# Order of a VectorE queue in the softmax rounds of a two-layer encoder trunk: maximum and preparation piece exchanged

## The reference

```python
def one_block(q_blk):                       # 2 blocks of 128 queries, 8 heads, 2 softmaxes (c)
    s = jnp.einsum('bqhcd,bkhcd->bhcqk', q_blk, k).astype(jnp.float32) * scale
    p = jax.nn.softmax(s, axis=-1)
    a = p[:, :, 0] - lam * p[:, :, 1]
    return jnp.einsum('bhqk,bkhe->bqhe', a.astype(v.dtype), v)
...
f = lb_dir + (1.0 - lb_dir) * jax.nn.sigmoid(f_raw)     # HGRN2, each of two directions
k, logf = heads(1.0 - f), heads(jnp.log(f))             # the scan then takes cumsum(logf)
```

## Time and profile before

| | |
|---|---|
| median of three executions | 2962.78 us (2958.91 to 2967.27) |
| profiled execution, time | 2959.23 us |
| profiled execution, span in the trace | 2957.4 us |
| TensorE busy | 2665.2 us, 90% of the span |
| VectorE busy | 1923.5 us, 65% |
| ScalarE busy | 1073.4 us, 36% |
| rounds 0 to 15 of the attention | from 616.71 us to 703.58 us of the span |

### The profile page before, as it was taken

One profiled execution on the slowest core, in us unless ns is written; L12 is line 12 of the kernel. 1 busy time (PEld: TensorE's weight loads), 2 busy tenths in 40 slices (PEclk: granted clock), 3 DMA queues, 4 the chain that ended last, 5 costly groups with the idle time before them and its releaser, 6 DMA issues.

```text
span 2957.4 us, 41913 instructions
## 1 busy us (share of the span) xinstructions
PE 2665.2 (90%) x16522; PEld 2154.3 (73%) x16522; DVE 1923.5 (65%) x1948; ACT 1073.4 (36%) x858; POOL 128.9 (4%) x201
## 2 busy tenths in 40 slices
PE   6969999976769899999999976859979999999997
PEld 3438888733458688888888862548868888888886
DVE  7956666657935777677777756746676665555555
ACT  3333333343223333333444422023433333344442
POOL 1020000000000200000000021010020000000000
PEclk9989999977879999999999988979989999999999
DMA  7988878622235488787878759468837777555551
GB/s 249 349 269 271 288 257 288 214 72 69 73 109 176 170 277 273 257 286 262 285 261 293 279 158 227 157 174 276 284 124 230 235 231 236 187 195 187 184 185 57
DMA packets 289270, 639.65 MB, mean 216 GB/s; under 512 B 76370, under 2 KB 79316, under 8 KB 285588
## 3 DMA queue, kind: packets, MB, share of 16 engines
q1 hardware_dynamic: 239236, 584.44, 59.7%
q0 software_dynamic: 11008, 35.99, 4.1%
q10 hardware_dynamic: 38928, 17.86, 2.2%
HBM read 614.24 MB, written 19.79 MB: 214 GB/s over the span
## 4 chain that ended last, share of the span: by engine, by line
PE 79%; DVE 12%; ACT 3%; ACTq 2%; issue 2%; DMA 1%; SPq 1%; DVEq 0%
PE PS L267 46%; PE PS L268 23%; PE PS L220 2%; ACT Pb L939 2%; DVE Pb L1693 2%; DVE acc L1688 1%; PE PS L885 1%; ACTq L983 1%; PE PS L184 1%; PE PS L714 1%; DMA omat<-WF 1%; DVE wlo L257 1%; DVE HF L1612 1%; ACTq L416 1%; PE PS L735 1%
## 5 line engine op out<-in xcount | busy, mean ns | idle before, releaser
L267 PE MATMUL PS<-H,whi 128*128 128x512 f32 x5888 | 2077.1, 398 | 102.0 <-DVE wlo L257 78.1
L268 PE MATMUL PS<-H,wlo 128*128 128x256 f32 x5888 | 1653.1, 281 | 0.0
L267 PEld LDWEIGHTS PS<-H,whi 128*128 128x128 f32 x5888 | 1112.3, 189 | 369.5 <-DVE wlo L257 84.5
L257 DVE TENSOR_TENSOR wlo<-raw,whi 128x2048 fp32r<-128x2048 f32 x368 | 843.6, 2293 | 735.3 <-ACT whi L253 734.8
L253 ACT ACTIVATE whi<-raw 128x2048 fp32r<-128x2048 f32 x368 | 705.3, 1918 | 1255.9 <-PE PS L268 1215.1
L268 PEld LDWEIGHTS PS<-H,wlo 128*128 128x128 f32 x5888 | 1118.6, 190 | 0.0
L176 DVE SCALAR_TENSOR_TENSOR acc<-araw,cact,acc 128x1024 f32<-128x1024 f32 x240 | 307.4, 1281 | 1.4 <-DMA araw<-in_ada_w 1.0
L939 ACT ACTIVATE Pb<-PS 128x1024 f32 (+5 forms) x117 | 118.3, 1035 | 162.1 <-issue 75.8
L939 ACT ACTIVATE H<-Pb 128x512 fp32r (+2 forms) x142 | 95.1, 670 | 41.6 <-DVE Pb L1358 27.7
L1406 DVE TENSOR_TENSOR H<-Pb,H 128x512 fp32r<-128x512 f32 x128 | 87.6, 684 | 0.0
L1302 DVE TENSOR_TENSOR raw<-Pb,HF 128x1024 f32<-128x1024 f32 x64 | 74.1, 1220 | 9.9 <-DMA omat<-WF 7.0
(11 more groups left out here) (258 smaller groups left out, 1406.0 us busy)
## 6 DMA issues: line engine op xcount, KB each, us to landing
raw<-in_mlp_w SPq DMA_DIRECT2D x256, 1024.0 KB, 5.8
araw<-in_ada_w SPq DMA_DIRECT2D x276, 512.0 KB, 4.5
raw<-in_mix_w_in SPq DMA_DIRECT2D x64, 1024.0 KB, 7.7
raw<-in_s_w_glu SPq DMA_DIRECT2D x32, 1024.0 KB, 7.4
acc<-in_ada_w SPq DMA_DIRECT2D x44, 512.0 KB, 7.0
raw<-in_ada_w POOLq DMA_DIRECT2D x32, 512.0 KB, 4.1
raw<-in_mix_w_out SPq DMA_DIRECT2D x16, 1024.0 KB, 5.1
vmat<-Pb ACTq DMA_DIRECT2D x8, 1024.0 KB, 7.5
```

The lines of the kernel that those rows point to most:

```text
L257: nc.vector.tensor_tensor(wlo[:, s % 2, :], raw[:, s, :], whi[:, s % 2, :].bitcast(F), ALU.subtract).then_inc(S("lo_done"), 1)
L267: nc.tensor.matmul(PS[:, b, :], w[0], H2[:, :, k, :], start=first, stop=False, skip_group_check=True)
L268: return nc.tensor.matmul(PS[:, b, 0:T], w[1], H2[:, 0, k, :], start=False, stop=last, skip_group_check=True)
```

## The change

The order of two calls in VectorE's loop over the rounds is exchanged. The instructions, their data and their semaphores stay the same. Maxima are taken in rounds 0 to 13 only; rounds 14 and 15 issue the same order as before.

```diff
             for n in range(16):
                 mix(n)
+                between(n)
                 if n < 14:
                     row_max(n + 2)
-                between(n)
```

## The result

The changed kernel took 2939.26 us in the median of 14 executions, the kernel before 2959.07 us in 14 beside it; the ratio is 0.9948, with a 95% interval of 0.9927 to 0.9968. That is 15.4 us less by the ratio (0.0052 x 2959), 19.8 by the medians. So the question is whether the rounds saved more than was worked out, whether something behind them saved too, or whether the absolute time was wrong for another reason.

A forecast was written before the change was run, and what follows sets the result against it. VectorE was taken as the loop of the rounds, with one trip to TensorE inside. Waits of 21.8 us gone less 8.9 new give 12.9 us; 2962.8 - 12.9 was rounded to 2950 us, range 2944 to 2959.

The forecast's parts named there:

- The bound and the trip: Rounds: VectorE is the loop with one trip to TensorE; covering it with the piece removes 14 waits, 20.2 us.
- The far bound of 0.60 us for the gap: Gap from mixing to piece: taken as 0.15 us each; at 0.60 it would cost 6.3 us more.
- The short covers: Rounds 0 and 1: the piece ends before the scores are ready, leaving waits of 0.60 and 0.75 us.
- TensorE keeps up: From round 2: TensorE's 3.53 us at full clock fits VectorE's shortest round of 3.77, 0.24 us to spare.
- The rule of the Trainium skill: Transposes do not engage the full clock; the rival with low clock throughout the rounds gives 2972 us, chance 0.03.
- The wait for the logarithms: At the piece of round 9: VectorE's wait for ScalarE's logarithms grows from 1.57 to 4.81 us.
- TensorE's late rest of round 9: After the logarithms: some 4 us of TensorE's low-clock work left; under 1 us might show, counted as nothing.
- The sum of the rounds: Up to the mixing of round 14: 21.8 us gone, 8.9 new, net 12.9 us.
- The shift goes through: Behind the rounds: the whole 12.9 us shift reaches the end; rival that it is given back, 2963 us, chance 0.09.
- the time that I give: Whole kernel: median of the runs, 2962.8 us, less 12.9, rounded to 2950 us; forecast's chance 0.74.

The follow-up runs named there:

- load: Two 4x256 products added on TensorE behind gate_part each round: on the changed kernel 2951.32 us, stage 76.6; on the kernel before 2961.31 us, stage 86.9.
- the last two experiments: On the changed kernel: round 9 left in the old order, 2932.69 us; ScalarE's logarithms moved behind the copy of round 9, median 2949.49 us, ratio 0.9959.
- the filler: Changed kernel with the clearing memset of round 15 issued 8 times instead of once, ahead of the first level: median 2961.68 us, ratio 1.0007.

## Why the prediction was wrong, point by point

**The bound and the trip: right.** VectorE was the loop with one trip to TensorE in it; 1.41 us from mixing to piece was forecast and measured, 3.77 us for the shortest round against 3.71. The far bound of 0.60 us for the gap appeared only where it was before, ahead of L1550.

**The short covers: right in place, 0.4 us too small.** Round 0 waited 0.71 us (0.60 forecast). Round 1 waited 1.05 (0.75), since `gate_part(0)`, where the clock rises, took 2.66 us instead of 2.32; over the six traces with the new order in round 0 and no load this wait lies between 0.81 and 1.30 us.

**TensorE keeps up: right.** The clock stayed up through rounds 2 to 8 and no maximum waited there. The shortest round left TensorE 0.20 us idle (at 654.94), where I had 0.24. The rule of the Trainium skill that spoke against it ("TensorE: Matmul & The Clock Gate", Part 4) did not decide: with two transposes among 14 matmuls the granted clock was 1.00 in rounds 2 to 8 and 0.89 over the stage, not 0.50. That the room hangs on the clock is shown by the run with only odd rounds exchanged: where the clock fell in an exchanged round, the next one gave 1.1 us back.

**The wait for the logarithms: right.** 4.81 us forecast, 4.96 measured. I let TensorE's late rest of round 9 cost nothing, which held only because the scans stand in front of the next maximum; the last two experiments showed that it is the bound there.

**The sum of the rounds: 12.9 us forecast, 13.04 measured. The shift goes through: right** as far as 14.0 +- 3.3 us over all executions and the filler can tell.

**The step that failed is the last one: "the time that I give is 2962.8 - 12.9, rounded to 2950".** The median of three executions was taken as the kernel's time, and "each median moves by some us by itself" was not put into the range in its full size. Over 53 executions the kernel before has a mean of 2956.9 us, 5.9 less than that median. Less the measured 13.0 it gives 2943.9, already at the low end of the range; the changed kernel's 36 executions have 2943.0, and the median of the first 14 lay another 3.7 us lower. So of the 10.6 us between the unrounded 2949.9 and the measured 2939.3, the base is 5.9, the size of the change 0.1, and 4.6 are scatter, 0.9 of the mean of the 36 and 3.7 of that first median. The mechanism and its size were right, the base of the sum was mis-sized by 6 us, and the spread around it was taken too small.

## What to carry to other kernels

An engine that waits for a short trip to another engine in each round can be given work of its own queue that needs nothing of that trip; what it saves is the trip less one gap for each round, as long as the other engine's own chain is shorter than the new round. Where that engine has two clocks, both lengths of its chain have to be held against the new round: here its 3.5 us fit, and the 5.1 us of a round in which the clock fell did not. Look next for a wait inside the moved piece: the later instruction is now queued behind it, and a long block on a third engine can show up as another wait where it is moved to, as it did here. And when a change is worth less than the scatter of whole executions, read its stretch of the trace, and take the base from as many executions as there are, not from three.

## What the runs showed of the hardware

Where a part of the scatter comes from was not expected. In the dense streams behind the rounds, with TensorE busy throughout and the granted clock at 1.00, the same code ran at one of two rates. Windows rows of 100 us (TensorE's busy us with its matmuls first; granted clock third from the end): the changed kernel, then the kernel with round 9 in the old order, then the kernel before in a later stream:

```profile
2420.00:2520.00 100.00, 100.00 (x568) 86.77 (x567) 61.78 (x37) 37.20 (x22) 0.00 (x0) 1.00 0.76 233
```

```profile
2420.00:2520.00 100.00, 100.00 (x579) 87.46 (x578) 63.46 (x38) 39.11 (x24) 0.00 (x0) 1.00 0.75 231
```

```profile
2800.00:2900.00 100.00, 100.00 (x579) 87.42 (x578) 52.24 (x37) 43.81 (x36) 0.00 (x0) 1.00 0.51 178
```

568 or 579 matmuls in 100 us, 1.9% apart: in nine such windows of each of ten traces every count is 567 to 570 or 577 to 579 (one window held a boundary with idle time and is left out). A stream of some 175 us is 3.3 us longer at the lower rate. The kernel before had the higher rate in 4 of its 9 windows, the first changed trace in 2, the kernel with round 9 in the old order in 7 of 8, and the latter two are the longest and the shortest behind L1581 (2267.6 and 2240.4 us). It is not the whole of the scatter: the kernel with the filler had the higher rate in 6 windows and took 2258.4 us there, the one with only odd rounds exchanged in 4, and took 2248.6. TensorE shows no idle time in these windows and the data rates are alike (233 and 231 GB/s), so nothing points to the loads. What picks the rate was not tried. Whether the new order shifts the odds can't be told either: 13.0 us lies within 14.0 +- 3.3.
